# Feed-forward of two blocks at once by seven products in place of eight, in a hybrid decoder layer on Trainium2

## What is computed

```python
h = modulate(rms_norm(x, norm1_g), shift1, scale1)
x = x + gate1 * token_mixers(h, ...)      # attention and gated DeltaNet, projections, output projection
h = modulate(rms_norm(x, norm2_g), shift2, scale2)
gate, up = jnp.split(h @ w_gate_up, 2, axis=-1)        # 1024 -> 2 x 2816
x = x + gate2 * ((jax.nn.silu(gate) * up) @ w_down)    # 2816 -> 1024
```

## Time and profile before

| | us |
|---|---|
| median of 3 runs | 3046.63 (3044.96 to 3048.59) |
| the profiled execution, its span | 3046.8 |
| TensorE busy | 3011.5 (99%) |
| VectorE busy | 1611.2 (53%) |
| ScalarE busy | 1205.2 (40%) |
| transfers | 356 MB, 117 GB/s mean |

### The profile page before, as it was taken

One profiled execution on the slowest core, in us unless ns is written; L12 is line 12 of the kernel. 1 busy time (PEld: TensorE's weight loads), 2 busy tenths in 40 slices (PEclk: granted clock), 3 DMA queues, 4 the chain that ended last, 5 costly groups with the idle time before them and its releaser, 6 DMA issues.

```text
span 3046.8 us, 39684 instructions
## 1 busy us (share of the span) xinstructions
PE 3011.5 (99%) x15810; PEld 2483.7 (82%) x15810; DVE 1611.2 (53%) x2584; ACT 1205.2 (40%) x1976; POOL 113.1 (4%) x110
## 2 busy tenths in 40 slices
PE   8999999999999999999999999999999999999999
PEld 6887878888798788888879778888887977888887
DVE  6876674333566667333365756633336575643333
ACT  4455443222356454222245544422224555432222
POOL 0011000000001100000000110000000011000000
PEclk9999999999999999999999999999999999999999
DMA  7433344323333433232343344323333333323233
GB/s 294 166 108 106 130 159 152 104 96 98 125 111 118 118 122 118 90 104 97 97 131 112 103 122 138 100 97 97 97 99 127 130 106 101 124 84 98 96 98 103
DMA packets 138008, 356.23 MB, mean 117 GB/s; under 512 B 38240, under 2 KB 38496, under 8 KB 134752
## 3 DMA queue, kind: packets, MB, share of 16 engines
q1 hardware_dynamic: 133472, 345.30, 35.0%
q10 hardware_dynamic: 4352, 8.39, 0.7%
HBM read 324.28 MB, written 29.36 MB: 116 GB/s over the span
## 4 chain that ended last, share of the span: by engine, by line
PE 87%; DVE 6%; ACT 2%; DVEq 2%; issue 1%; DMA 1%; POOL 0%; SPq 0%
PE gb L1819 69%; PE gb L2178 5%; PE gb L1847 4%; PE mb L2023 2%; DVE w_lo L1177 1%; PE mb L2018 1%; PE mb L1996 1%; PE mb L1929 1%; ACT sc L969 1%; DVE tmp_c L1490 1%; DVE inv_c L1493 1%; DVE n_acc L1184 1%; PE mb L2089 0%; ACT sc L961 0%; PE mb L2090 0%
## 5 line engine op out<-in xcount | busy, mean ns | idle before, releaser
L1819 PE MATMUL gb<-h_hi,w_hi 128*128 128x512 f32 x2432 | 956.4, 393 | 1.8 <-DVE w_lo L1177 1.2
L1819 PE MATMUL gb<-h_lo,w_hi 128*128 128x512 f32 x2432 | 954.3, 392 | 0.0
L1819 PE MATMUL gb<-h_hi,w_lo 128*128 128x512 f32 x2432 | 954.1, 392 | 0.0
L771 ACT ACTIVATE w_hi<-w_raw 128x1024 fp32r<-128x1024 f32 x488 | 514.5, 1057 | 1023.2 <-PE gb L1819 976.5
L1177 DVE TENSOR_TENSOR w_lo<-w_raw,w_hi 128x1024 fp32r<-128x1024 f32 x488 | 595.7, 1222 | 473.4 <-ACT w_hi L771 471.9
L1819 PEld LDWEIGHTS gb<-h_hi,w_hi 128*128 128x128 f32 x2432 | 457.2, 188 | 103.9 <-issue 5.8
L1819 PEld LDWEIGHTS gb<-h_lo,w_hi 128*128 128x128 f32 x2432 | 457.6, 188 | 99.2 <-issue 6.9
L1819 PEld LDWEIGHTS gb<-h_hi,w_lo 128*128 128x128 f32 x2432 | 457.4, 188 | 95.3
L1819 PE MATMUL gb<-hid_hi,w_hi 128*128 128x512 f32 x704 | 274.0, 389 | 0.0
L1819 PE MATMUL gb<-hid_hi,w_lo 128*128 128x512 f32 x704 | 273.9, 389 | 0.0
L1819 PE MATMUL gb<-hid_lo,w_hi 128*128 128x512 f32 x704 | 273.9, 389 | 0.0
(11 more groups left out here) (293 smaller groups left out, 3374.6 us busy)
## 6 DMA issues: line engine op xcount, KB each, us to landing
w_raw<-in_wstream SPq DMA_DIRECT2D x488, 512.0 KB, 3.7
ada_buf<-in_ada_w SPq DMA_DIRECT2D x24, 1024.0 KB, 7.8
x<-in_x SPq DMA_DIRECT2D x4, 2048.0 KB, 10.3
out<-x ACTq DMA_DIRECT2D x16, 512.0 KB, 3.4
xs<-in_x SPq DMA_DIRECT2D x12, 512.0 KB, 5.3
scratch_nt<-st_nt SPq DMA_DIRECT2D x16, 256.0 KB, 2.6
scratch_at<-st_at SPq DMA_DIRECT2D x16, 256.0 KB, 2.9
scratch_kd<-st_kd SPq DMA_DIRECT2D x16, 256.0 KB, 3.1
```

The lines of the kernel that those rows point to most:

```text
L771: act.activation(w_hi[s][:, :], w_raw[s][:, :], ACT.Copy).then_inc(w_high.sem, 1)
L1819: last = pe.matmul(bank(j), w, r, start=(i == 0), stop=(i == n - 1))
```

## The change

The feed-forward leaves the per-block loop. Blocks 0 and 1 are done as before up to `x1`, which is parked in DRAM (`park_x`); after block 1 the feed-forward of both runs at once, and the same for blocks 2 and 3. Two 2x2 block products are each done with seven products (Winograd's form of Strassen's scheme):

- **Gate and up.** For hidden tile i the 2x2 of weights is (gate, up) x (contraction half 1, 2), that of activations (half 1, 2) x (block one, block two). The sums of activations t1 to t4 are formed once per pair, the sums of weights (p = 5, 6, 3, 7) per tile by VectorE (`weight_sum`). A product has four contraction tiles and three passes, 12 matmuls of 128x512. Products 6, 3, 7 and 4 add to a bank that holds an earlier one; ScalarE keeps copies (`keep_product`), VectorE adds them to `c_sum`, ScalarE applies Silu (`open_gate`), VectorE multiplies. 22 x 7 = 154 steps.
- **Down.** The 2x2 of weights is (output half 1, 2) x (even, odd hidden tiles), that of activations (even, odd) x (block one, two). After every second hidden tile VectorE forms seven tiles, the products' and their sums (`hidden_sums`), in `spill`, and SP sends them to DRAM (`park_t`, 7 x 256 KB). Down goes product by product (1, 2, 6, 5, 7, 3, 4), each over the 11 pairs: 77 steps of 12 matmuls, each with one hidden tile loaded again from DRAM through six buffers and split anew, and one 128x512 weight part from the four quarters `wq` in SBUF, summed by VectorE for p = 6, 7, 3 (two additions for 6 and 3). `add_down` adds four banks at a product's end to the residual `xd`, loaded back from DRAM.
- Weight parts are now 128x512, in six buffers (`PARTS`), split by ScalarE (`high`) and VectorE (`low`).
- The next block's input norm is moved: that of blocks 1 and 3 stays in the output projection of blocks 0 and 2; in blocks 1 and 3 its place is taken by the norm of the other block's parked `x1`; that of block 2 runs inside down (steps 60 to 76). The two early DeltaNet units and `keep_warm` at that place go.
- All modulation pieces from 4 on are summed by VectorE, four in block 0's chunk loop and four in block 1's.

The core of the diff:

```diff
+def gate_order():
+    order = [(i, p) for p in (1, 2, 5, 6, 3, 7, 4) for i in range(2)] + [(2, 1)]
+    for i in range(2, NFT):
+        order += [(i, 5), (i, 2), (i, 6), (i, 3), (i, 7)]
+        if i + 1 < NFT:
+            order.append((i + 1, 1))
+        order.append((i, 4))
+    return order
+DOWN_PRODUCTS = (1, 2, 6, 5, 7, 3, 4)
+PARTS, W_AHEAD, T_RING = 6, 3, 5
-ADA_ROWS = (0, 1, 2, 3, 8, 9)
+ADA_ROWS = (0, 1, 2, 3)
...
 @block.sync
+                for step in range(N_DOWN_STEPS):
+                    if step == 0:
+                        sp.wait_ge(spilled.sem, spilled.at(be, 16 * (NPAIR - 1)))
+                    if step == NPAIR - 1:
+                        sp.wait_ge(spilled.sem, spilled.at(be, 16 * NPAIR))
+                    if step >= 6:
+                        sp.wait_ge(t_ready.sem, t_ready.at(be, step - 5))
+                    load_hidden(step)
+                    if step in (1, 3):
+                        load_down(0, (step + 1) // 2)
+                    if step == 5:
+                        sp.wait_ge(spill_ready.sem, spill_ready.at(be, NPAIR))
+                        sp.dma_start(park_t[be][NPAIR - 1], spill[:, 0:7, :]).then_inc(spilled.sem, 16)
+                        sp.wait_ge(p_used.sem, p_used.at(be, N_GATE))
+                    if step in (6, 7, 8):
+                        load_down(1, step - 6)
+                    if step in (9, 20, 24, 40):
+                        load_residual((9, 20, 24, 40).index(step))
+                    if step in (11, 13, 15):
+                        load_down(2, (step - 11) // 2)
+                    if step in (16, 17, 18):
+                        load_down(3, step - 16)
...
 @block.scalar
+            def token_high(b, step):
+                be, k = b // 2, raw_slot(step)
+                act.wait_ge(t_loaded[k].sem, t_loaded[k].at(be, 16 * (step // 6 + 1)))
+                if step < T_RING:
+                    act.wait_ge(p_used.sem, p_used.at(be, GATE_AT[NFT - 1, 3] + 1))
...
 @block.vector
+                dve.wait_ge(stored.sem, stored.at(b + 1, 0))
+                for k in range(5):
+                    if k < 4:
+                        norm_scale(which, k, x1[:, k, :])
+                        dve.drain()
+                        dve.tensor_tensor(t_tmp[k % 2][:, :], x1[:, k, :], xs[:, k, :], ALU.subtract).then_inc(tk_raw.sem, 1)
+                    if k:
+                        tile_low(be, 5, k - 1)
+                weight_sum(b, 6)
+                weight_sum(b, 7)
+                low(b, 6)
+                low(b, 7)
+                for k in range(5):
+                    if k < 4:
+                        norm_scale(which, 4 + k, x1[:, 4 + k, :])
+                        dve.drain()
+                        dve.tensor_tensor(x1[:, k, :], x1[:, 4 + k, :], x1[:, k, :], ALU.subtract)
+                        dve.drain()
+                        dve.tensor_tensor(xs[:, k, :], x1[:, k, :], xs[:, k, :], ALU.add).then_inc(tk_raw.sem, 1)
+                    if k:
+                        tile_low(be, 6, k - 1)
...
+                for n in (2, 3, 8, 9, 10, 11):
+                    after_step(b, n)
+                weight_sum(b, 15)
+                seen = 12
+                for n in range(14, N_STEPS):
+                    for k in range(seen, n - (PARTS if n < N_GATE else T_RING) + 1):
+                        after_step(b, k)
+                        seen = k + 1
+                    ...
+                    low(b, n)
+                    if step >= 0:
+                        token_low(b, step)
+                    if n + 2 < N_STEPS:
+                        weight_sum(b, n + 2)
...
 @block.tensor
+                pe.wait_ge(n_ready.sem, n_ready.at(rank_of(N_NEXT[b]), KD))
+                for n in range(4):
+                    for k in range(4):
+                        gate_product(b, n, k)
+                    if n == 1:
+                        norm_stat(N_OUT[b])
+                    if n == 2:
+                        norm_spread(N_OUT[b])
+                for place in range(5):
+                    for k in range(4):
+                        pe.wait_ge(tk_ready.sem, tk_ready.at(be, 4 * place + k + 1))
+                        gate_product(b, 4 + 2 * place, k)
+                        gate_product(b, 5 + 2 * place, k)
+                for n in range(14, N_GATE):
+                    for k in range(4):
+                        gate_product(b, n, k)
```

More of the change, by code:

```diff
@@ L745, in _ @@
                     out_power(c)
[L747 to L748 removed]
+                norm_power(N_NEXT[b])
+                if b % 2:
+                    norm_power(N_OUT[b])
+                if b == 1:
+                    norm_power(N_DOWN)
         @block.scalar
@@ new lines, in hidden_sums, with add_down @@
+            def hidden_sums(be, q):
+                b11, b21, b22, t1, t2, t3, t4, b12 = [spill[:, k, :] for k in range(8)]
+                dve.drain()
+                dve.tensor_tensor(t3, b22, b12, ALU.subtract)
+                dve.tensor_tensor(t1, b12, b11, ALU.subtract)
+                dve.drain()
+                dve.tensor_tensor(t2, t3, b11, ALU.add)
+                dve.drain()
+                dve.tensor_tensor(t4, b21, t2, ALU.subtract).then_inc(spill_ready.sem, 1)
+            def add_down(be, p):
+                first = 4 * DOWN_PRODUCTS.index(p)
+                side, row, k = {1: (0, 0, 0), 2: (0, 0, 0), 6: (1, 0, 1), 3: (1, 0, 1), 5: (1, 4, 2), 7: (1, 4, 2),
+                                4: (0, 4, 3)}[p]
+                dve.wait_ge(xd_in[k].sem, xd_in[k].at(be, 16))
+                dve.drain()
+                for j in range(4):
+                    if p == 4 and j < 3:
+                        dve.wait_ge(d_last.sem, d_last.at(be, j + 1))
+                    elif p == 4:
+                        dve.wait_ge(p_used.sem, p_used.at(be, N_STEPS))
+                    tile = xd[:, side, row + j, :]
+                    dve.scalar_tensor_tensor(tile, flat_bank((4 if p in (2, 5, 3) else 0) + j), mod_g[:, 1, row + j:row + j + 1],
+                                             tile, ALU.mult, ALU.add).then_inc(d_evac.sem, 1)
@@ L1727, in _ @@
+                if b < LAST:
+                    split(b + 1, 0)
+                for k in range(seen, N_STEPS):
+                    after_step(b, k)
+                if b < LAST:
+                    split(b + 1, 1)
         @block.tensor
@@ L1855, in turn_qk, with product @@
                 pe.transpose(m(1)[:, 0, :], qk[:, HEADS * HEAD_DIM:QKW], ident[:, :]).then_inc(qk_turned.sem, 1)
+            def product(out, k, tile, hi, lo, c, first, last):
+                for part in range(3):
+                    w = (fw_lo if part == 2 else fw_hi)[k][:, c * P:c * P + P]
+                    done = pe.matmul(out, w, (lo if part == 1 else hi)[:, tile, :] if tile is not None else (lo if part == 1 else hi),
+                                     start=(first and part == 0), stop=(last and part == 2), skip_group_check=True)
+                return done
@@ L2221, in _ @@
[L2221 to L2236 removed]
+                if b % 2 == 0:
+                    continue
```

967 lines of the change are left out of this document (660 added, 307 removed).

## The result

The changed kernel takes 2924.98 us (median of 4 runs, 2923.94 to 2927.59) against 3046.57 of the kernel before (4 runs, 3044.96 to 3048.59) on the same chip: a ratio of 0.9598, 95% interval 0.9586 to 0.9609. The profiled execution has a span of 2922.2 us, 124.6 less than the one of before. The forecast was 2940, in a range of 2905 to 2985.

The account below looks back on a forecast made before the run. The prediction took TensorE, busy 99% of the span, as the bound. A credit of 192.2 us less 85.6 us of losses left 106.6 net, taking 3046.8 to 2940 us, in a range of 2905 to 2985.

Parts of the forecast that it names:

- the burst: Start of down: spill, weights, residual and hidden tiles share one queue at 300 GB/s, so tiles come late; 7 us a pair.
- the two-sum product: Down, p = 6: VectorE just at TensorE's pace, no lead left, four bank additions fall into it; 4 us a pair.
- between the pairs: Scaling tiles of block 2 ends 1 us before TensorE does; 1 us lost, once.
- Credit: Gains from 792 fewer matmuls, the last block's gap, exposed statistics and moved modulation; 192.2 us.
- Ramp: Start of each pair: TensorE follows VectorE's queue through fourteen steps, ending at 64.1 instead of 38.1; 26.0 us a pair.
- The clock term: In each ramp, two waits of 5 to 6 us may slow the matmuls behind them; 2 us a pair.
- Gate to down: Handover from gate stage to down: TensorE waits for ScalarE's copy and for c22 of tile 21; 3.3 us a pair.
- Rival B: Burst and two-sum product cost nothing because small tiles overtake large loads; 2918, or 2905 with shorter ramps; chance 0.15.
- A: The forecast itself: VectorE paces the ramps and the burst costs some; 2918 to 2962 us; chance 0.58.
- Rival C: VectorE bounds down too, two-sum steps take 3.06 us, lead is lost in the gate stage; 2970 to 3000; chance 0.23.
- rival D: Slower than before: hidden tiles come late from scratch in down, landings over 12.1 us slow the steps; chance 0.02.
- Rival E: Products run but every group of tiles waits for the last, so only the gap is gained; near 3045; chance 0.02.

Follow-up runs that it names:

- e1_warm: The changed kernel plus 20 spare 128x512 matmuls into an unused bank ahead of the t4 products in each ramp; 2923.89 us, ratio 0.9591.
- e4_burst: The changed kernel plus a 2 MB copy inside DRAM in SP's queue, behind the last spill and ahead of the hidden tiles; 2941.44 us, ratio 0.9653.
- e3_down_load: The changed kernel plus one unused 0.60 us VectorE operation in each of steps 20 to 30 of down; 2933.67 us, ratio 0.9626.
- e5_gate_load: The changed kernel plus one unused 0.60 us VectorE addition in each of 140 gate-stage passes a pair; 2926.18 us, ratio 0.9602.
- e2_c22_first: The changed kernel with VectorE's order turned: c22's sums first, those ending in the first hidden sum two passes earlier; 2918.35 us, ratio 0.9576.
- e8_burst1: The changed kernel plus a 0.5 MB copy inside DRAM behind each pair's last spill, ahead of the hidden tiles; 2929.87 us, ratio 0.9618.

## Why the prediction was right, and where it was not

It had the direction, the bound (TensorE) and the mechanism of the largest loss, the ramps that VectorE's queue paces, and came out 15 us above the median, 18 above the profiled span. Two of the losses that it added, the burst and the two-sum product, did not appear; with the 1 us between the pairs they are 23 of its 85.6 us. Part of that was made good by luck: ramps and handovers cost 9.2 us more than forecast. Step by step:

- **Credit, right.** The pace of 0.2267 us stands: 36 matmuls of the gate stage took 8.16 us, as 36 x 0.2267. The gap of the earlier trace rows is gone.
- **Outside the feed-forward, 3.6 us too little.** The forecast had 1.5 us from the moved modulation, and 3.4 from two statistics and spreads that leave these stretches: 4.9. Without the matmuls of the feed-forward, and without the 665.6 us of the first pair, the four stretches of the table changed by -4.9, +0.6, -5.3 and +1.1: 8.5 us shorter. Some 1.5 of the 3.6 are the modulation: block 1's chunk loop, where VectorE now does the four pieces, grew from 46.0 to 46.7 us (517.0 to 563.7), so the sums cost 0.7 there and not 2.2. One execution differs from the next by some us at these points, and the rest stays open.
- **Ramp, 26.0 + 2 for the clock forecast, 31.4 measured in both pairs.** Each point from the scaling to c22 came 0.45 to 2.3 us later than forecast, a slip that adds up in VectorE's queue. The step that failed is "the next steps are ready by then": step 14 waited for the first hidden sum, and `e1_warm` shows that this wait, not the clock, sets the end. The clock term had the right sign in the trace and no price: 0 at this place. The forecast's own sign, 61 to 68 us to the end of these steps, was missed with 69.5, though not its outer bounds of 55 and 75.
- **Gate to down, 3.3 forecast, 3.7 and 5.3 measured.** The two waits are the named ones; the second pair's 1.6 us more are matmuls at a low clock, which the forecast had put only in the ramps.
- **The burst, 7 a pair forecast, 0 measured.** The order in the queue was right (`e4_burst`), the rate was not. I took 300 GB/s from a row with 292 at a share of 0.78 and said that this queue was kept full. It was not: at its share the same row gives 292 / 0.78 = 374 for a full one, and the full one here moved 414. At 374 tile 9 would have landed at 21.8, in time. Tile 9 was forecast to land 25.6 us after down begins and landed after 20.8. The Trainium skill (DMA: Bandwidth & Descriptors, Measured) gives 425 GB/s for a load of 16 MB; the mean of 414 here is within 3% of it, and the sum that I had worked out from it, 14 us lower, was the better one. Rival B had the price right and gave the wrong reason.
- **The two-sum product, 4 a pair forecast, 0 measured.** This hung on the burst: with no lead lost there, VectorE enters it ahead, and 6.6 us of added work in `e3_down_load` cost 3.2 and 3.8.
- **Between the pairs, 1 forecast, 0 measured.** The next block's first unit starts at 1484.88 with the last product of down just out.

The sizes close: -14 for the burst, -8 for the two sums, -1 between the pairs, +6.8 for the ramps, +2.4 for the handovers are -13.8, and -3.6 from outside the feed-forward makes -17.4, of 18.0 seen (124.6 against 106.6). The clock term is counted within the ramps. The chances do not quite close: with B, A and half of C in the range, the rivals leave 0.155 outside and not 0.18. The single largest error was the queue's rate. Rival C fails by `e5_gate_load` (0.60 us of further work a pass is free) in the gate stage and by two-sum steps of 2.76 us, rival D by landings with a median of 11.5 us in the burst and of 3.1 on the page: single ones took up to 15.5, over its 12.1, but none stood in TensorE's way. Rival E fails by the gate stage without a gap.

## What to carry to other kernels

A row with a rate is a ceiling only if its share of busy time is near one: divide by the share before you use it (here that gave 374, still 10% under what a full queue moved). Where the engine that paces a ramp works through one queue, follow this queue one entry past the last wait that you found, for the next entry takes that wait's place. And before you accept a ramp, look where the pacing engine itself stands waiting ahead of it: moving sums there, with the better order of `e2_c22_first`, took 24 of the 63 us that the two ramps lost, with no work removed.

## What the runs showed of the hardware

- A lower clock need not cost anything. After a wait of 5.6 us the granted clock was at 0.50 (1.2 GHz) from 881 to 885 us, at 0.91 in the next 4 and then full; with it kept up by spare matmuls the ramps were no shorter (69.1 and 68.8 us against 68.6) and the ratio was the same (0.9591 and 0.9598). The Trainium skill (TensorE: Matmul & The Clock Gate, Part 1) has the throttled state as what activity releases; the trace agrees, at both waits of the ramp.
- Where no other engine was behind, it did cost: after the waits of 4.1 and 5.4 us in `e4_burst` the next twelve matmuls took 1.5 and 2.5 us more than at full clock, and the whole of it reached the end.
- A copy inside DRAM of 2.1 MB held back what stood behind it in the queue by 7.0 to 8.0 us, one of 0.5 MB by 2.0 to 2.3: 230 to 300 GB/s, where loads to SBUF moved 414 in the same queue.
- At the handover the same twelve matmuls took 3.00 us in one pair and 4.58 in the other, after the same waits of 1.4 and 1.8 us. It differs from run to run: the low clock was there in the second pair of the changed kernel, in the first of `e8_burst1`, in both of `e4_burst` and in neither of `e1_warm`. Each time it costs 1.6 us.
